# Hybrid decoder step on one core: the sample cache in whole pages, fetched behind the sum of the pair in front

## The reference

```python
past = cache_nsa_kv[l][page_table].reshape(Bd, past_len, 4, NSA_KV, NSA_HD)   # k_cmp, v_cmp, k_slc, v_slc
s = jnp.einsum('bqgrd,bngd->bqgrn', q, kc_blk)      # means of 32 k_cmp rows; p @ v_cmp means
s = jnp.einsum('bqgrd,bgqsd->bqgrs', q, kg)         # k_slc of the selected blocks; p @ v_slc
# window: q against k_win, p @ v_win, over win_prev and the new rows
```

## Time and profile before

| | |
|---|---|
| time, median of 3 executions | 2237.5 us (2236.99 to 2238.45) |
| profiled execution: time | 2235.7 us |
| profiled execution: span of its instructions | 2234.1 us |
| PE busy (matmuls) | 2039.3 us, 91% |
| DVE, ACT, POOL busy | 770.1, 540.4, 83.5 us |
| mean granted TensorE clock | 0.962 of full speed |
| DMA, mean over the span | 76 GB/s |

### The profile page before, as it was taken

One profiled execution on the slowest core, in us unless ns is written; L12 is line 12 of the kernel. 1 busy time (PEld: TensorE's weight loads), 2 busy tenths in 40 slices (PEclk: granted clock), 3 DMA queues, 4 the chain that ended last, 5 costly groups with the idle time before them and its releaser, 6 DMA issues.

```text
span 2234.1 us, 27892 instructions
## 1 busy us (share of the span) xinstructions
PE 2039.3 (91%) x10568; PEld 1539.4 (69%) x10568; DVE 770.1 (34%) x1898; ACT 540.4 (24%) x1162; POOL 83.5 (4%) x121
## 2 busy tenths in 40 slices
PE   1898989999799999999929999899997999999996
PEld 1576779887575566777717777789875655677775
DVE  1245633332255433411113273423224444433111
ACT  1013330201526621100020324211114465211000
POOL 0000100101010000000000001000010100000000
PEclk9899999998899999999959999999988999999998
DMA  4221410201431035431141114011124101454211
GB/s 173 101 62 51 99 38 20 39 20 62 124 97 35 5 112 157 139 108 57 38 146 59 57 57 98 20 39 20 62 58 131 61 29 38 145 172 123 58 56 62
DMA packets 185909, 169.08 MB, mean 76 GB/s; under 512 B 48224, under 2 KB 181650, under 8 KB 184998
## 3 DMA queue, kind: packets, MB, share of 16 engines
q1 hardware_dynamic: 181558, 147.85, 22.5%
q0 software_dynamic: 4208, 19.36, 2.5%
HBM read 151.36 MB, written 24.07 MB: 79 GB/s over the span
## 4 chain that ended last, share of the span: by engine, by line
PE 86%; DVE 5%; ACT 3%; issue 2%; DMA 2%; SPq 2%; DVEq 0%; POOL 0%; ACTq 0%
PE PS L756 55%; PE PS L703 5%; PE PS L906 2%; PE PS L921 2%; PE PS L1092 2%; PE PS L1105 2%; PE PS L920 2%; DMA arena<-in_x_sample 1%; PE PS L1171 1%; PE PS L1161 1%; PE PS L990 1%; PE PS L794 1%; PE PS L1038 1%; PE PS L841 1%; PE PS L814 1%
## 5 line engine op out<-in xcount | busy, mean ns | idle before, releaser
L756 PE MATMUL PS<-hT,ring 128*128 128x288 f32 x3968 | 1081.0, 414 | 26.9 <-ACT arena L1307 8.8
L756 PEld LDWEIGHTS PS<-hT,ring 128*128 128x128 f32 x3968 | 730.8, 193 | 230.3 <-issue 24.0
L703 PE MATMUL PS<-con,arena 128*128 128x128 f32 (+4 forms) x942 | 147.3, 284 | 94.6 <-DMA arena<-in_nsa_k_norm 38.9
L703 PEld LDWEIGHTS PS<-con,arena 128*128 128x128 f32 (+4 forms) x942 | 111.8, 143 | 150.4 <-issue 73.5
L756 PE MATMUL PS<-zs,owr 128*128 128x288 f32 x768 | 211.7, 409 | 0.0
L756 PEld LDWEIGHTS PS<-zs,owr 128*128 128x128 f32 x768 | 141.4, 190 | 40.5 <-issue 4.6
L756 PE MATMUL PS<-arena,ring 128*128 128x288 f32 x512 | 124.6, 406 | 2.3 <-DVE arena L1552 2.3
L756 PEld LDWEIGHTS PS<-arena,ring 128*128 128x128 f32 x512 | 97.1, 190 | 29.8 <-issue 3.1
L1325 ACT ACTIVATE sg<-PS 128x288 f32<-128x288 f32 x96 | 38.7, 404 | 289.3 <-PE PS L756 289.3
L1590 DVE SCALAR_TENSOR_TENSOR arena<-arena,par 128x512 f32<-128x512 f32 x192 | 99.5, 518 | 6.8
L1632 DVE SCALAR_TENSOR_TENSOR mpr<-sg,PS 128x288 f32<-128x288 f32 x64 | 29.1, 454 | 208.7 <-PE PS L756 206.1
(11 more groups left out here) (288 smaller groups left out, 1851.0 us busy)
## 6 DMA issues: line engine op xcount, KB each, us to landing
ring<-in_w_in SPq DMA_DIRECT2D x54, 1024.0 KB, 5.5
arena<-in_cache_nsa_kv SPq DMA_DIRECT2D x128, 192.0 KB, 2.5
ring<-in_w_in SPq DMA_DIRECT2D x32, 256.0 KB, 4.2
arena<-in_state_nsa_win SPq DMA_DIRECT2D x32, 256.0 KB, 3.2
arena<-in_cache_nsa_kv SPq DMA_DIRECT2D x128, 64.0 KB, 1.8
ring<-in_w_out SPq DMA_DIRECT2D x8, 1024.0 KB, 5.0
out_win_sample<-in_state_nsa_win POOLq DMA_DIRECT2D x2, 4032.0 KB, 25.5
xs<-arena SPq DMA_DIRECT2D x2, 2304.0 KB, 7.3
```

The costliest lines, as they stand in the source:

```text
L703: return nc.tensor.transpose(dst, src, ident[0:src.shape[0], 0:src.shape[0]])
L756: ins = mm(dst, w, x, start=i == 0, stop=i == len(steps) - 1)
```

## The change

Pages and windows are no longer split into keys and values. `cached` loads a whole page with one DMA (`ck_in`), `window` a whole window with one (`wk_in`), and `cv_in` is gone with the wait on it. For pairs 1 to 3 both are issued behind `s_pv` of the pair in front, and the wait for `s_t` is gone. Per layer there are 64 transfers of pages of 256 KB where there were 64 of 192 KB and 64 of 64 KB, and 8 of windows where there were 16.

```diff
--- before.py
+++ after.py
@@ -260,7 +260,7 @@
 par_in lrow_in w_in0 w_in1 ow_in0 ow_in1 par_t sq_ok ms_ok rstd_ok h_ok pj pa pv lam_ok lh_t u_ok lgp
 lg at_ok lt_ok lq_ok lru_ok lc_ok lc_in lo_t lo_ok gt_t gt_ok gs_ok nq_y nq_sw nq_r qk_ok kt_t kt_e vc_mm
 c_ok c_s c_m c_e c_t c_c c_pv c_n a_s a_m a_p a_r a_n a_t a_ca a_cd a_v z_o
-qb_ok ck_in wk_in cv_in s_pl s_pe s_kt s_ke s_t s_ed s_ea s_sg s_sc s_pv s_cm s_ce
+qb_ok ck_in wk_in s_pl s_pe s_kt s_ke s_t s_ed s_ea s_sg s_sc s_pv s_cm s_ce
 s_cn s_im s_wc s_m s_mw s_wm s_sm s_p s_pw s_tr s_tb s_ta s_mix s_or s_ot s_z dr_in dh_t
 conv_ok silu_ok dc_ok sp_abs sp_exp gb_ok n_ok s0_in p_z p_y p_g p_e p_x p_s p_d p_k p_b i_w
 i_wm i_x i_xm f_mm f_u f_v f_w m_mm u_mm f_m q_w q_s q_n q_oe b_gl b_pe b_so b_vt
@@ -529,22 +529,14 @@
                     at_page = sp.value_load(pgt[0:1, b * PAGES + k:b * PAGES + k + 1], min_val=0, max_val=N_PHYS - 1)
                     return pages[bass.ds(sp.snap(at_page + l * N_PHYS), 1)].rearrange("a p c -> (a p) c")
 
-                def cached_keys(k2):
+                def cached(k2):
 
                     for b in (2 * k2, 2 * k2 + 1):
                         for k in range(PAGES):
-                            sp.dma_start(page(b % 2, k)[:, 0:3 * P], page_of(b, k)[:, 0:3 * P]).then_inc(s["ck_in"], 16)
-
-                def cached_values(k2):
-                    for b in (2 * k2, 2 * k2 + 1):
-                        for k in range(PAGES):
-                            sp.dma_start(page(b % 2, k)[:, 3 * P:4 * P], page_of(b, k)[:, 3 * P:4 * P]).then_inc(s["cv_in"], 16)
-
-                def window_keys(b):
-                    sp.dma_start(win[b % 2][:, :, 0:P], wins[b][:, :, 0:P]).then_inc(s["wk_in"], 16)
-
-                def window_values(b):
-                    sp.dma_start(win[b % 2][:, :, P:2 * P], wins[b][:, :, P:2 * P]).then_inc(s["cv_in"], 16)
+                            sp.dma_start(page(b % 2, k), page_of(b, k)).then_inc(s["ck_in"], 16)
+
+                def window(b):
+                    sp.dma_start(win[b % 2], wins[b]).then_inc(s["wk_in"], 16)
 
                 weights(0)
                 weights(1)
@@ -565,26 +557,19 @@
                 weights(20)
                 sp.wait_ge(s["st_ok"], 1)
                 sp.wait_ge(s["dn_ok"], 1)
-                cached_keys(0)
-                window_keys(0)
-                cached_values(0)
-                window_values(0)
+                cached(0)
+                window(0)
                 for g in (21, 22, 23, 24):
                     weights(g)
                     out_weights(g - 19)
                 sp.wait_ge(s["a_p"], N_UNIT)
-                window_keys(1)
-                window_values(1)
+                window(1)
                 for k2 in range(DEC_BATCH // 2):
                     if k2 < DEC_BATCH // 2 - 1:
-                        sp.wait_ge(s["s_t"], 6 * (k2 + 1))
-                        cached_keys(k2 + 1)
+                        sp.wait_ge(s["s_pv"], k2 + 1)
+                        cached(k2 + 1)
                         for b in (2 * k2 + 2, 2 * k2 + 3):
-                            window_keys(b)
-                        sp.wait_ge(s["s_pv"], k2 + 1)
-                        cached_values(k2 + 1)
-                        for b in (2 * k2 + 2, 2 * k2 + 3):
-                            window_values(b)
+                            window(b)
                     weights(25 + k2)
                     out_weights(6 + k2)
                 sp.wait_ge(s["s_pv"], DEC_BATCH // 2)
@@ -1237,7 +1222,6 @@
                     turn(PS[0:2 * NPB, 6, 2 * P:3 * P], cp2).then_inc(s["s_m"], 1)
                     fill(2, end)
 
-                    pe.wait_ge(s["cv_in"], 16 * 2 * (PAGES + 1) * (k2 + 1))
                     pe.wait_ge(s["s_mix"], k2 + 1)
                     pe.wait_ge(s["s_tb"], k2 + 1)
                     for k in range(PAGES):
```

## The result

The changed kernel takes 2327.28 us (median of 4 executions, 2325.32 to 2328.64), the kernel before beside it 2237.82 us (median of 4, 2236.99 to 2238.45): 89.5 us more, a ratio of 1.0399 with a 95% interval of 1.0381 to 1.0417. The prediction was 2331 us in a range of 2314 to 2352.

The account below looks back on a forecast made before the run. PE's own time was taken as the bound, so late loads are paid in full. Six times a 12.7 us wait plus 2.85 us of low clock gave 93.3 us over the kernel before, 2331 us, range 2314 to 2352.

Parts of the forecast that it names:

- The bound: In layer 0's pairs PE is busy 159.03 of 160 us, so a load later than PE wants is paid in full.
- Fewer transfers gain nothing: On SP's queue, 128 fewer issues at 1.13 us save 145 us of SP's time, all hidden behind PE.
- The wait of 12.7 us, six times: PE waits for the late page fetch before pooling in pairs 1 to 3 of both layers, 76.2 us in total.
- T: The end of the last matmul of a pair's sum, from which the next fetch's times are counted.
- The landing: Time for a 256 KB page to arrive after its issue, taken as 2.7 us before PE begins to pool.
- The pace of issue decides most: SP's gap between page issues: 1.0 or 1.25 us instead of 1.13 moves the time by 11 us.
- The clock, 2.85 us each: Behind each of the six waits PE runs at 1.2 GHz for 5.7 us, half lost: 17.1 us in all.
- the rival that the clock costs little: Low clock behind each wait costs only 1.4 us, 6 x (12.7 + 1.4) = 85 us, 2322 us; chance 0.07.
- Windows and weights behind the pages cost nothing: Windows queued behind the pages land by about T + 25, wanted at T + 29.4; weights are for two pairs later.
- The backlog of the DMA engines: DMA engines become the bound in the page fetch and the last page lands late: 2351 to 2354 us; chance 0.09.
- stay low beyond the pooling: Clock at 1.2 GHz up to the first window's transposes, costing 8.7 us more per pair: 2366 us; chance 0.06.
- The rival of the other sign: Not slower: whole pages issue fast enough to hide the fetch before pooling, 2234 to 2237.5 us; chance 0.04.

Follow-up runs that it names:

- Two of the three parts of the change, tried alone: Against the kernel before: whole pages fetched early, 2237.38 us, ratio 1.0003; whole windows of pairs 1 to 3 fetched behind the sum, 2236.12 us, ratio 0.9997.
- the third alone: Kernel before with the next pair's keys of pages and windows fetched behind the sum, transfers split as before: 2325.84 us, ratio 1.0400.

## Why the prediction was right

- *The bound.* PE's own time with no room under it: right. Two of the three parts of the change, tried alone, were free (ratios 1.0003 and 0.9997), and the third alone gave the whole loss (1.0400).
- *Fewer transfers gain nothing*: right, as the whole pages fetched early show.
- *The wait of 12.7 us, six times.* Measured 13.15, 78.9 us in all. Term by term: the first issue at T + 0.77 for 0.86, the last 16.9 us behind it for 17.1, and from there to PE's start 3.6 us for 2.7. The landing is the term that was too small. The prediction took it from medians, and PE waits for the last page, which lands in 3.3 to 3.9 us where the median page takes 2.9.
- *The pace of issue decides most*: right. With half of the gap the loss falls to 52 us, with 1.5 times the gap it rises to 138 us. What makes the gap was read too simply: the prediction gave all of it but the DMA instruction's 0.33 us to reading the page number. With the numbers read ahead, 0.57 us are left, so the read and its arithmetic are 0.55, and the other 0.24 stay.
- *The clock, 2.85 us each.* The mechanism is shown (with PE kept busy the pooling is at full speed), the term was too large: 10.9 / 6 = 1.8 us, nearer to the 1.4 of the rival that the clock costs little. The low level held for 4.4, 3.6 and 2.8 us behind the three waits of layer 0, where the row that was chosen had 5.7 and the other one 2.8. The two errors, +2.7 us on the waits and -6.2 on the clock, cancel in part, which is why the median came out only 3.5 us under the forecast. That closeness is in part luck; the rival's 2322 us was 5 us off.
- *Windows and weights behind the pages cost nothing*: right, no wait names them, and the windows alone were free.
- *The rivals.* The backlog of the DMA engines did not come at 1.12 us per page, but is there at 0.57, where whole pages land in 4.7 us instead of 2.9. The clock did not stay low beyond the pooling (at most 4.4 us in layer 0, where the pooling took 5.8). The rival of the other sign, whole pages that go out fast, failed on the gap: even at 0.57 us PE waits for 6.9 us.

## What to carry to other kernels

A transfer is worth moving, merging or splitting by what it does to the moment when it can start. Merging two fetches whose buffers come free at different times ties both to the later one, and here that cost 4% while halving the number of transfers gained nothing, since the issuing queue had slack and PE had none. Before such a change, count the time between the event that frees the last byte and the first reader. Set against it the first issue, the gaps times their number, and the landing of the last transfer, which may be slower than the median. Add what the low clock behind the wait costs. Where a fetch must be late, take out of its gap what doesn't depend on the event (here the reads of the page table), and let the reader start on the part that lands first, without breaking up work that runs side by side.

## What the runs showed of the hardware

Reading a page number from SBUF with its register arithmetic costs SP 0.55 us of a 1.12 us gap between two page DMAs of 256 KB (0.57 without it, 1.67 with two). With one read the gap is 1.12 to 1.13 us whether the DMA moves 64, 192 or 256 KB.

Matmuls with 32 output columns that alternate between two places in PSUM's partitions take 3.65 us for 32 records of the trace (16 matmuls), and 3.64 for 16 records when they go to one place only. The Trainium skill describes this packing: matmuls whose outputs start at different ones of the partitions 0, 32, 64 and 96 run at the same time in different parts of the array ("TensorE: Matmul & The Clock Gate", Part 3: Packing small matmuls). By that rule, the trace agrees: 32 records against 16 in the same 3.6 us. Splitting a loop by sample undoes it unseen, and here it cost 8 x 3.64 = 29 us.

How long the low clock lasts behind the same wait differs between executions of the same instructions. The changed kernel has the instructions of before in its first stage, with the same wait of 8.78 us. Behind it, from 76.63 us, it held the low level until 81.8 us, that is for 5.1 us. The kernel before held it from 77.14 until 80.0, for 2.8 us. The windows of both, after first:

```profile
80.00:84.00 4.00, 4.00 (x14) 1.69 (x13) 0.74 (x7) 0.00 (x0) 0.00 (x0) 0.78 0.70 297
```

```profile
80.00:84.00 4.00, 4.00 (x18) 1.86 (x17) 1.14 (x9) 0.00 (x0) 0.00 (x0) 1.00 0.87 371
```

Half of the difference is lost time, so a clock term read from one execution has an uncertainty of about a microsecond for each wait.
